# Hyena projections interleaved with the filter spectrum, and modulation chunks computed in two other places

## The reference

```
sh1, sc1, g1, sh2, sc2, g2 = split(silu(c) @ w_mod + b_mod, 6)      # w_mod 1024 x 6144; also for c_ctx, of which sh1, sc1 are used
h  = rms_norm(x, norm1_g)   * (1 + sc1)  + sh1                      # 1024 tokens
hc = rms_norm(ctx, norm1_g) * (1 + csc1) + csh1                     # 256 context tokens
qa, ka, va, hy, qd, kd, vd = split(h @ w_in)                        # also hc @ w_in, for the keys and values
q, k = rope(rms_norm(q)), rope(rms_norm(k))                         # per head of 64; context keys without rope
filters = FFN(sin features) * decay / L1 norm                       # 1024 x 2 directions x 2 orders x 256
v, x1, x2 = split(dwconv3(hy), 3)                                   # depthwise, width 3
yh = x2 * long_conv(x1 * long_conv(v, filters[0]), filters[1])      # FFT convolutions
... attention with q, k, v; merge; output projection, x + g1 * y
h = rms_norm(x, norm2_g) * (1 + sc2) + sh2                          # then the gated FFN, x + g2 * ...
```

## Time and profile before

| | |
|---|---|
| median of 3 runs (lowest, highest) | 3981.91 us (3981.68, 3983.74) |
| profiled execution | 3986.07 us, its span 3984.8 us |
| TensorE busy | 3565.9 us, 89% |
| VectorE, ScalarE, GpSimd busy | 1331.1, 903.7, 245.4 us |
| chain that ended last, by engine | PE 79%, DVE 12%, ACT 6% |
| stages, by TensorE's order of time | front to 182.1, projections to 280.4, convolutions to 446.4, q/k/v to 777.8 us |

### The profile page before, as it was taken

The page is one execution under the profiler, slowest core; times in us unless marked ns, Lnnn a source line. Parts: engine busy times, 40 slices in busy tenths (PEclk is TensorE's granted clock), DMA queues, the critical chain, the costliest instruction groups (busy, mean ns, idle before and its releaser), DMA issues.

```text
span 3984.8 us, 30565 instructions
## 1 busy us (share of the span) xinstructions
PE 3565.9 (89%) x12486; PEld 1959.5 (49%) x12486; DVE 1331.1 (33%) x2454; ACT 903.7 (23%) x1725; POOL 245.4 (6%) x236
## 2 busy tenths in 40 slices
PE   8797799899998999999999999999789978999991
PEld 4356554666663444444444456765357434444440
DVE  6748345255551111111100023213656141111116
ACT  1210145267762100000000012112334031111112
POOL 0002111000000000000000000000000002222213
PEclk9898999999999999999999999999999988999996
DMA  4225200000002110110011100002000118888874
GB/s 178 74 95 192 104 21 22 32 1 1 1 1 95 43 42 32 43 40 31 29 44 37 55 32 27 32 10 85 11 12 10 44 69 332 329 330 329 328 291 153
DMA packets 59785, 362.24 MB, mean 91 GB/s; under 512 B 6442, under 2 KB 12858, under 8 KB 33020
## 3 DMA queue, kind: packets, MB, share of 16 engines
q1 hardware_dynamic: 37036, 179.39, 12.4%
q0 software_dynamic: 22608, 180.89, 12.1%
HBM read 325.03 MB, written 35.22 MB: 90 GB/s over the span
## 4 chain that ended last, share of the span: by engine, by line
PE 79%; DVE 12%; ACT 6%; issue 1%; DMA 1%; POOL 0%; SPq 0%; DVEq 0%; ACTq 0%; POOLq 0%
PE ps L1150 15%; PE ps L2241 8%; PE ps L1197 8%; PE ps L1306 5%; PE ps L2258 4%; PE ps L764 4%; PE ps L915 3%; PE ps L1900 3%; PE ps L1095 3%; PE ps L1308 3%; PE ps L890 3%; PE ps L664 2%; PE ps L767 2%; PE ps L603 2%; PE ps L1740 1%
## 5 line engine op out<-in xcount | busy, mean ns | idle before, releaser
L1150 PE MATMUL ps<-arena 128*128 128x512 f32 x1408 | 606.3, 593 | 5.0 <-ACT arena L1136 5.0
L1150 PEld LDWEIGHTS ps<-arena 128*128 128x128 f32 x1408 | 268.1, 190 | 343.0 <-issue 337.3
L2241 PE MATMUL ps<-arena 128*128 128x512 f32 x752 | 332.1, 594 | 0.0
L1197 PE MATMUL ps<-arena 128*128 128x512 f32 x704 | 302.4, 591 | 1.4 <-DVE arena L1183 1.4
L2241 PEld LDWEIGHTS ps<-arena 128*128 128x128 f32 x752 | 139.7, 191 | 159.1 <-issue 159.1
L2258 PE MATMUL ps<-arena 128*128 128x512 f32 x376 | 174.0, 605 | 48.6 <-DVE arena L2309 48.6
L2199 POOL DMA_INDIRECT arena<-in_wgu_dram,arena x47 | 44.1, 939 | 2807.0 <-DVE arena L2160 2562.4
L1197 PEld LDWEIGHTS ps<-arena 128*128 128x128 f32 x704 | 132.8, 189 | 171.0 <-issue 168.8
L1306 PE MATMUL ps<-arena 128*128 128x512 f32 x480 | 211.0, 600 | 0.0
L764 PE MATMUL ps<-arena 128*128 128x512 f32 (+1 forms) x432 | 174.9, 558 | 7.8 <-DMA arena<-in_win_a_dram 7.8
L915 PE MATMUL ps<-arena 128*128 128x64 f32 (+1 forms) x1280 | 162.4, 283 | 8.2 <-ACT arena L957 5.3
(11 more groups left out here) (331 smaller groups left out, 4669.9 us busy)
## 6 DMA issues: line engine op xcount, KB each, us to landing
arena<-in_wmod_dram SPq DMA_DIRECT2D x24, 1024.0 KB, 4.9
yslot<-arena SPq DMA_DIRECT2D x47, 512.0 KB, 7.9
arena<-in_wup_dram SPq DMA_DIRECT2D x22, 1024.0 KB, 4.8
arena<-in_wout_dram SPq DMA_DIRECT2D x16, 1024.0 KB, 4.8
arena<-in_cf_dram SPq DMA_DIRECT2D x12, 1024.0 KB, 5.0
arena<-in_wdn_dram SPq DMA_DIRECT2D x16, 704.0 KB, 4.0
arena<-in_w2b_dram SPq DMA_DIRECT2D x9, 1024.0 KB, 4.8
arena<-in_ci_dram SPq DMA_DIRECT2D x8, 1024.0 KB, 6.9
```

The lines of the kernel that those rows point to most:

```text
L1150: ins = mm(bk(b + tc), sb(wat(n) + k * 256 + which * 128, 128), sb(HT + k * 1024 + tc * 512, 512), k == 0, k == 7)
L1197: ins = mm(bk(bs[tc]), sb(wat(n) + k * 128, 128), sb(GB + (11 * hh + k) * 1024 + tc * 512, 512), hh == 0 and k == 0, hh == 1 and k == 10)
L2241: ins = mm(bk(b), sb(XB + i % 2 * 1024 + k * 128, 128), sb(WGU[i % 3] + k * 512, 512), k == 0, k == 7)
```

## The change

1. **Early modulation.** Chunks 0 to 7 are all computed by `pe_mod_direct`, into different columns of bank 6, and one VectorE instruction adds their bias (`dve_mod_first`). Chunk 0 stands where it was, chunk 1 behind norm 0, chunk 2 behind norm 1, chunks 3 to 7 behind the filter products of blocks 3 to 7.
2. **Norms.** TensorE's sums of squares of the three norms come ahead of the filter blocks; ScalarE's squares around the second Sin. VectorE's mean squares stand at the start and behind blocks 1 and 4, its normalisations behind blocks 0, 2 and 5.
3. **Loads.** cz comes ahead of cons, all of x ahead of fw3 and the context, chunks 1 and 2 behind these.
4. **Spectra.** The filter spectra (`pe_kf`, `act_kf`, `dve_kf`) leave the front: each stands behind two Hyena projections, the fourth between the turns of tiles 4 and 5. The projections use banks 4 to 7. The context is modulated between spectra 2 and 3.
5. **Late modulation.** Chunks 8 to 23 leave the projections and convolutions and stand among the 57 q/k/v jobs (`mod_at`). They have one buffer of their own (WM), reloaded when VectorE's sums of the chunk before are done; SyncE issues four of the win_d chunks and four wout chunks between them.
6. **q/k/v.** The rotation comes at step i+3 rather than i+2, from three buffers; projections have four banks, sums two (4, 5), rotations one (6), bank 7 the late chunks.
7. `stat` gives the same places by another expression.

```diff
-WLIST = ([("cz", 1), ("wmod", 4)] + [("cf", 1), ("wmod", 1)] * 4 + [("win_hy", 1), ("wmod", 1), ("win_hy", 1), ("wmod", 2), ("win_hy", 1), ("wmod", 2)]
-         + [("cf", 1), ("wmod", 1)] * 4 + [("ci", 1), ("wmod", 1)] * 4 + [("cf", 1), ("wmod", 1)] * 3 + [("cf", 1)] + [("ci", 4)]
+WLIST = ([("cz", 1), ("wmod", 8)] + [("win_hy", 1), ("cf", 1)] * 2 + [("win_hy", 1), ("cf", 2)]
+         + [("cf", 4), ("ci", 4)] * 2
...
     def dve_mod_sums(i):
-        n = nth["wmod"][i]
         V.wait_ge(*(yield ("silu",)))
-        V.wait_ge(*wready(n))
+        V.wait_ge(lmod, 16 * (i - 7))
+        if i > 9:
+            V.wait_ge(*(yield ("modp", i - 2)))
...
     def sp_front():
         LD.ready()
         dma.dma_start(out=sb(M_P, NP_), in_=X["params"]).then_inc(*LD.turn(("params",)))
+        yield from sp_weights(0, 1)
         LD.ready()
         dma.dma_start(out=sb(M_C, NC_), in_=X["cons"]).then_inc(*LD.turn(("cons",)))
-        yield from sp_weights(0, 2)
+        yield from sp_weights(1, 2)
+        for k in range(4):
...
     def pe_front():
...
         ins.then_inc(*P.step(("f2",)))
         held[2] = held[3] = [("sine", 2)]
+        yield from pe_normalise(0)
+        yield from pe_mod_direct(1)
+        yield from pe_normalise(1)
         yield from pe_mod_direct(2)
-        yield from pe_mod_sum(1)
+        yield from pe_normalise(2)
...
             held[b] = held[b + 1] = [("decay", j)]
+            if j > 2:
+                yield from pe_mod_direct(j)
             if j:
                 yield from pe_l1(j - 1)
...
     def dve_front():
...
-            if j == 3:
-                yield from dve_mod_bias(3)
+            if j in (1, 4):
+                yield from dve_mean_square((j + 2) // 3)
+            if j in (0, 2, 5):
+                yield from dve_normalise((j + 1) // 3)
+        yield from dve_mod_first()
...
     def pe_conv(o):
...
-            if (o, kt) < (1, 3):
-                yield from pe_mod_step(5 + 8 * o + kt)
...
     def pe_hyena():
...
+        for c in range(3):
+            yield from pe_hy_proj(2 * c)
+            yield from pe_hy_proj(2 * c + 1)
+            yield from pe_kf(c)
+            if c < 2:
+                yield from pe_hy_turn(2 * c)
+                yield from pe_hy_turn(2 * c + 1)
+        yield from pe_hy_turn(4)
+        yield from pe_kf(3)
         yield from pe_hy_turn(5)
...
+    mod_at = [4, 8, 12, 16, 20, 24, 28, 32, 36, 39, 42, 45, 48, 51, 53, 55]
+
     def sp_qkv():
...
-        yield from sp_weights(nth["win_a"][0], nth["wout"][4])
+        yield from sp_weights(nth["win_a"][0], nth["win_d"][2])
+        n = nth["win_d"][2]
+        for i in range(8, 24):
+            if i > 8:
+                S.wait_ge(*(yield ("macc", i - 1)))
+            else:
+                S.wait_ge(*(yield ("convd", 1, 3, 1)))
+            dma.dma_start(out=sb(WM, 2048), in_=X["wmod"][i]).then_inc(lmod, 16)
+            if i in (8, 12, 13, 14, 15, 16, 20, 23):
+                yield from sp_weights(n, n + 1)
+                n += 1
 
     def pe_qkv():
-        projb, sumb, rotb = ring([0, 1, 2]), ring([3, 4]), ring([5, 6])
+        projb, sumb, rotb = ring([0, 1, 2, 3]), ring([4, 5]), ring([6])
...
-            if is_rope(i - 2):
+            if is_rope(i - 3):
...
+            if i - 3 in mod_at:
+                yield from pe_mod_sum(8 + mod_at.index(i - 3))
...
     def dve_qkv():
...
+            if i - 4 in mod_at:
+                yield from dve_mod_bias(8 + mod_at.index(i - 4))
+            if i - 1 in mod_at:
+                yield from dve_mod_sums(8 + mod_at.index(i - 1))
```

More of the change, by code:

```diff
@@ L226, in build @@
     yf = sb(YF, 4096).rearrange("p (d k c) -> p d k c", d=4, k=4)
[L227 to L230, removed]
+    macc = {i: M_S + 188 + 256 * (i % 2) for i in range(8, 24)}
+    WM = BIG + 31168
+    lmod = nc.alloc_semaphore("late_mod")
     def pe_mod_direct(i):
         n = nth["wmod"][i]
-        yield from claim(6)
         P.wait_ge(*(yield ("silu",)))
@@ L302, in pe_normalise, with dve_mean_square @@
         held[b] = [("nx", q)]
[L304 to L313, removed]
+    def dve_mean_square(q):
         src, c0, n, width, parts = norms0[q]
@@ L522, in dve_front, with act_squares @@
             vt.tensor_scalar(xx, xx, sb(AMUL + 2 * k + 1, 1), modv[:, 0, k, 1:2], MUL, ADD).then_inc(*V.step(("hc",)))
+    def act_squares(q):
+        src, c0, n, width, parts = norms0[q]
+        for k in range(8):
+            A.wait_ge(*(yield ("x", k * parts // 8) if parts > 1 else ("cx",)))
+            if q or k > 1:
+                A.wait_ge(*(yield ("sumsq", q - (k < 2), (k - 2) % 8)))
+            st.activation(sb(SQ0 + k % 2 * 512, n), sb(src + k * width + c0, n), ACT.Square).then_inc(*A.step(("square", q, k)))
     def act_front():
@@ L653, in pool_conv, with pe_hy_proj @@
             gt.tensor_tensor(yf[:, 1, kt], u[2], u[3], SUB).then_inc(*G.step(("prod_pool", o, kt)))
+    def pe_hy_proj(f):
+        n, b = nth["win_hy"][f // 2], hybank(f)
+        P.wait_ge(*wready(n))
+        yield from claim(b, b + 1)
+        for tc in range(2):
+            for k in range(8):
+                ins = mm(bk(b + tc), sb(wat(n) + k * 256 + f % 2 * 128, 128), sb(HT + k * 1024 + tc * 512, 512), k == 0, k == 7)
+        ins.then_inc(*P.step(("hyproj", f), *([("w", n)] if f % 2 else [])))
+        held[b] = held[b + 1] = [("hycopy", f)]
     def pe_hyena():
@@ L817, in dve_qkv @@
         V.wait_ge(*(yield ("prod_pool", 1, 3)))
-        for i in range(NJ + 2):
+        for i in range(NJ + 3):
             if is_qk(i - 1):
@@ L1006, in dve_combine @@
         V.wait_ge(*(yield ("exp", i, 1)))
[L1007 removed]
+        vt.reciprocal(stat(i, "rec0", 2), stat(i, "sum0", 2)).then_inc(*V.step())
         if units[i][0] == "d":
```

269 lines of the change are left out of this document (120 added, 149 removed).

## The result

The changed kernel takes 3996.3 us (median of 20 runs, 3978.4 to 4004.4), the kernel before 3983.8 us beside it (3981.1 to 3987.2); the ratio is 1.0025, 95% interval 1.0013 to 1.0036. So it is slower by 12 us where 11.5 us faster was forecast, and lies above the range. The profiled run took 4001.5 us, 5.3 above the median; its span is 15.4 us longer than that of before, and the table splits these 15.4 us.

What follows compares the result with a forecast made beforehand. VectorE's serial chains were taken to bound the first 446 us, TensorE's own work most of the next 331. Terms -49.8 + 44.8 - 26.5 + 20 = -11.5 us took 3981.91 to 3970.4 us; range 3943 to 3991.

Steps and rivals of the forecast that it cites:

- The front: Stage before the first Hyena projection: projections start at 132 us, 50 earlier (term -49.8 us).
- L1 and filter 6.1 us, chunk 5.0: Filter loop on TensorE: price of a round's L1 sum with filter, and of its direct chunk.
- the swing: Filter loop: each two-column chunk lets TensorE's clock fall again; chunk 5.0 us, L1 and filter 6.1 us.
- rival (b): Filter loop: clock hardly rises between chunks, costing up to 32 us, total up to 4002 us; chance 0.1.
- its bound of 164: Front: latest projection start, 164 us, if TensorE's clock is never at the upper level.
- the fast case: Front: clock stays up through direct chunks, projections start at 107 us, 25 earlier, total 3945.4 us; chance 0.17.
- Projections: Hyena projections with filter spectra and turns: 143 us, all TensorE, 44.8 us longer than the 98.3 before.
- convolutions: Two long convolutions: spectral tiles on VectorE at 8.06 us instead of 12.03; stage 26.5 us shorter.
- Q/k/v: q/k/v projections: late chunks' work, stalls and restarts make the stage 20 us longer, bounds 12 and 33.
- 3 us of restarts at the lower level: q/k/v stage on TensorE: 3 us for restarts at the lower clock, part of the 20 us longer.
- Rival (c): Late chunks cost more, through reload sharing queues with win_d or GpSimd multiplying beside sums: 13 us more, 3983.4 us; chance 0.15.
- Attention and later unchanged: From attention on, the change leaves every instruction as it was; forecast difference 0 us.

Runs made afterwards that it cites:

- The wide run: Changed kernel with the products of the eight direct modulation chunks taking 128 columns instead of two; 3962.7 us (ratio 0.9952).
- the run with two buffers: Changed kernel with 128-column direct products, plus two transfer buffers instead of one for the late chunks; 3950.1 us (ratio 0.9916).
- the fastest kernel: Changed kernel with 128-column direct products, chunks 3-7 two rounds earlier, late chunks moved out of q/k/v, two rotation banks, first q/k/v weights requested earlier; 3922.2 us (ratio 0.9845).

## Why the prediction was wrong

**The front (missed by 10.6 us).** The order of events was right: VectorE's normalisation 0 holds the second L1 sum, and a chunk of two columns lets the clock fall. The step that failed is the price of a round, "L1 and filter 6.1 us, chunk 5.0". It took the swing for certain, and the loop went through without any fast row: L1 and filter 7.0, chunk 6.7 us. This is rival (b), told in the prediction with its place and given 0.1; alone it would have left the kernel about as fast as before, and the sign turned only with q/k/v. The trace of before had rows for it that the prediction didn't use, an L1 sum and a filter slow throughout behind a wait:

```profile
45.26 3.78 PE L395 MATMUL ps<-arena 128*128 128x512 f32 x4 [3.33 <-ACT arena L535]
48.83 3.62 PE L421 MATMUL ps<-arena 65*128 65x512 f32 x4
```

The start lies at 142.9 between the forecast's 132 and its bound of 164, since chunks 1 and 2 and the loop to 59 us were fast. Luck had a part in the small miss: the second L1 sum began at 67.0 instead of 71.3 us, which took 4.3 us off; it and its filter cost 0.8 more, five chunks and four pairs 61.3 us instead of 49.4, and from the last chunk to the projection it was 7.6 us instead of 5.3, because the two last L1 sums (6.7 us) had been left out of the count. The wide run also corrects the bound on the other side: 107 us was put down as "always the upper level", and 103.8 was measured.

The Trainium skill, "TensorE: Matmul & The Clock Gate", Part 1, has the clock follow how busy the engine has been. Here the trace disagrees: 29.7 us of chunks without a pause, begun at 1.00, ended at 0.50. The prediction had weighed this rule and rightly not followed it, but gave the fast case a higher chance (0.17) than the slow one (0.1), though its own eight slow filter rows at 34.75 us pointed the other way.

**Projections (143.4 for 143) and convolutions (139.7 for 139).** Both are sums of rows of before, and both held. Two neighbouring spectral tiles on VectorE, which answer to the earlier trace rows, lie 8.06 us apart, as forecast:

```profile
301.87 0.41 DVE L351 TENSOR_TENSOR arena<-ps,arena 128x256 f32<-128x256 f32 x1
...
309.93 0.41 DVE L351 TENSOR_TENSOR arena<-ps,arena 128x256 f32<-128x256 f32 x1
```

**Q/k/v (missed by 10).** The waits were right in sum: 19.3 + 0.6 = 19.9 us before, 23.2 + 3.7 + 3.3 + 0.3 + 0.6 = 31.1 after, 11.2 more where 34.7 - 24.0 = 10.7 had been carried through; the cause at the rotation was L851 as named, 23.2 us for "about 25". The added work is 5.9 us at the upper level, as priced. The step that failed is the term "3 us of restarts at the lower level". TensorE's busy time in the stage rose from 303.7 to 322.4 us: 18.7, of which 5.9 is work, so 12.8 us are rows at the lower level (granted clock 0.94 for the stage, 0.98 before). Behind the stalls at jobs 8 and 9, for instance, sixteen rows take 3.62 us, where 64 of the same kind take 7.39 a little later:

```profile
501.08 2.08 PE L798 MATMUL ps<-arena 128*128 128x512 f32 x2 [4.40 <-DVE arena L851]
502.95 3.62 PE L780 MATMUL ps<-arena 128*128 128x128 f32 x16
508.71 1.13 PE L798 MATMUL ps<-arena 128*128 128x512 f32 x2 [2.14 <-DVE arena L851]
...
516.49 7.39 PE L780 MATMUL ps<-arena 128*128 128x128 f32 x64
```

The rise in waits of 11.2 us was priced, the slow rows behind them hardly. Their price isn't fixed. The kernel with wide products has the same q/k/v program:

```profile
394.90:745.50 350.60, 317.86 (x1076) 194.49 (x1076) 182.82 (x327) 126.22 (x166) 28.57 (x22) 0.96 0.22 80
```

Its waits there are 12.8 us above those of before (32.7 for 19.9), and its busy time 14.2, so 8.3 us of slow rows go with them. In the kernel before with the later rotation and two banks the waits are 11.6 us shorter (8.3 for 19.9) and TensorE is busy for 4.0 us less. So a microsecond of waiting went with 0.35 to 1.1 us in slow rows, and 3 us was too little by any of the three. Rival (c) has the stage and the size (13 us), but not this reason. That the reload of the one buffer mattered was in the sum, and the run with two buffers bears it out.

**Behind q/k/v (missed by 5.8).** "Attention and later unchanged" holds for the instructions, not for their time. The step that failed is the 0. The first 62.6 us of attention were at clock 0.92 before and at 0.82 after (last stretch above), where TensorE comes in from the waits for the last sums. Up to the first product of the output projection attention takes 3.7 us more; the other 2 us weren't traced to a place. That these waits are the cause isn't shown: in other runs this part lay between 3208.7 and 3213.0 us, and it took 3213.0 us in the fastest kernel, which has no late chunk ahead of attention.

**What stayed open.** Why the loop stays at the lower level in one kernel and rises in each round of the other isn't settled. An 8.1 us wait stood ahead of the one and none ahead of the other, but the same program came out of this wait with a filter of 3.62 us in one run and of 2.66 in another. The changed kernel's times spread over 26 us in 20 runs, against 6 before: five lie at 3978.4 to 3979.7 us with a mean granted clock of 0.959 to 0.960, below every one of the kernel before, and six at 4000 us or above with 0.952 to 0.954. So the difference between these runs goes with TensorE's clock. That the five had the swing in the filter loop would fit, but five rounds at 3.3 us are 16.5 of the 22 us, and only a run of 4001.5 us was traced, so this is argued, not shown.

## What to carry to other kernels

Work moved from VectorE to TensorE as products of two columns costs more than its own rows where the clock falls in it, since all the work around it pays; look for a row of that form begun at the upper level, or measure one, before counting on either price, and try it with more columns, which cost almost nothing here. Work put beside a stage is free only if that stage has idle time on the engine and the bounding engine asks for the result a tile later (13.7 us of waits became 1.2). Price a new stall at its length and the slow rows behind it: here a third to a little more than the whole of its length again.

## What the runs showed of the hardware

- Direct products of 128 and of 2 columns take nearly the same time at the upper level (3.73 and 3.63 us a chunk), but with 128 the granted clock was 1.00 from the first chunk to the last (66.6 to 98.0 us), and with 2 it fell to 0.50 within a stretch in which TensorE was never idle.
- The loop with narrow chunks was seen in two patterns, 10.34 and 13.65 us a round, each over several rounds, with the same instructions of TensorE in each round and no wait in either (granted clock 0.67 and 0.50).
- The times of one program spread over 26 us in 20 runs (3978.4 to 4004.4), and the mean granted clock went with them, from 0.960 to 0.952.
